# Squares summed as they arise, h made in pieces and halved HGRN exponents in a hybrid SSD / HGRN2 / S5 / MoE layer

## The chip, the cores and the metric

The kernel runs on one core of a Trainium2 chip. The metric is device time in microseconds (us) for one call. The core's engines work side by side, each through its own instructions in order, and wait for each other on semaphores: PE (TensorE, matrix products and transposes), DVE (VectorE), ACT (ScalarE), POOL (GpSimd), and SP, which here only issues DMA transfers. All data is float32. PE's records come in pairs: one 128x320 product in the program is two MATMUL records in the trace.

## The reference, cut to what matters

One layer, with 256 prompt tokens and 64 sample tokens of width 2048, 320 in all. The parts that this change touches:

```python
def rmsnorm(x, g):
    xf = x.astype(F32)
    y = xf * lax.rsqrt(jnp.mean(xf * xf, axis=-1, keepdims=True) + EPS)
    return (y * g.astype(F32)).astype(x.dtype)

# chunk_gla, 64 tokens per chunk; HGRN has a decay per key, SSD one per head
b = jnp.cumsum(lc, axis=1)
diff = b[:, :, None] - b[:, None, :]
dec = jnp.where(causal[...], jnp.exp(jnp.minimum(diff, 0.0)), 0.0)
scores = jnp.einsum('bthk,bshk,btshk->btsh', qc, kc, dec)        # HGRN

# mixer
y_a = y_a.reshape(bsz, t, SSD_WIDTH) * jax.nn.silu(z.astype(F32))
out_a = rmsnorm(y_a, P['ssd_norm_g'][l])                         # the SSD norm
merged = jnp.concatenate([out_a, out_b, out_c], axis=-1)
mix = merged @ P['w_out'][l]

# trunk
x = x + gt1 * m
h = rmsnorm(x, P['g_ffn'][l]) * (1 + sc2) + sh2                  # the second norm (n2)
x = x + gt2 * hmoe(h, P, l)                                      # router, 32 experts, top 2 of one group
```

## The kernel before, in words

Activations lie with channels on the partitions and the 320 tokens along the free dimension: `xT` and `hT` are 16 tiles of 128 x 320. A table, `PLAN`, written out by rules in `make_plan`, sets one order of work for PE, and from it `act_order` makes the order of ACT and DVE. The heavy input projections (L1066), the modulation products (L965) and the parts of the output projection that don't need SSD (L1099) are laid as filler between the steps of S5, HGRN and SSD, so that PE has something to do while DVE and ACT prepare a step. Since PE works strictly in order, a step whose operands come late stops the filler behind it too.

**HGRN.** Two pairs of heads, seven levels each. At level 0 a masked product of q and k gives the diagonal. At each of the levels m = 32, 16, 8, 4, 2, 1 (`hg_level`) the tokens fall into blocks of 2m; only pairs with the query in a block's later half and the key in its earlier half count, and a mask (`lmask`) drops all others. DVE makes, over all 640 columns (two heads x 320), the difference of the running sum `hb` to the block's reference column (L1772) and the smaller of it and its negative (L1773); ACT takes the exponential (L781); DVE multiplies q (L1776) and k (L1777) with it, and PE forms the scores (L1172).

**SSD.** Five chunks of 64 tokens. For each, PE makes the decays (L1263, `ssd_decay`), DVE and ACT the weights, and PE the output (L1271, L1282, L1287, `ssd_y`). DVE gates it into `proj`, tiles 0 to 7 (L1947, semaphore `ssd_done`). When all five are done, and POOL has added the last filler piece to `xT` (`x_part` 16), ACT squares the eight tiles two at a time into the two halves of `sq` (L673) while PE sums them over the partitions with a matrix of ones (`sum_squares`, L956). DVE makes the mean (L1537), ACT the root, DVE the reciprocal (L1541) and the normed tiles (L1954).

**Output projection and second norm.** PE then runs 16 tiles of 8 products (L1345) with four PSUM banks in rotation; after each tile DVE adds it to `xT` (L2001, `x_mixed`). ACT squares pairs of tiles of `xT` into `sq`, which has two places. They are released by PE's `sum_squares`, and that stands behind the whole output projection. After it come the mean, the root, the reciprocal, four small operations that make the scale (1 + sc2) g (L1552, L1553, `modulate`), four multiplications of four tiles each (L1546, `scale_x`), and the shift: ACT does the prompt columns of each tile (L684), DVE the 64 sample columns (L1557). The router's 16 products (L1354) each need one finished tile of `hT`. Behind them follow the choice of experts, the gather of tokens, and 16 pairs of experts, whose weights SP loads as places come free.

## Time and profile before

| | us |
|---|---|
| median of 3 runs | 1496.92 (1494.64 to 1498.01) |
| the profiled execution's own time | 1496.93 |
| its span in the trace | 1495.0 |
| PE busy | 1224.5 (82%) |
| DVE busy | 520.3 (35%) |
| ACT busy | 197.6 (13%) |
| POOL busy | 261.6 (18%) |

The share of each engine is an average over stages with different limits. HGRN lies between about 381 and 634 us, SSD between 636 and 765, the output projection from 765 to 837, the second norm and the router from 837 to 869, the choice of experts up to 904, and the experts from 904 to 1406. The time outside the span is 1.9 us.

### The profile page before, as it was taken

The numbers are of one execution on the slowest core, as the hardware profiler recorded it, in microseconds if no ns is written. First come the engines' busy times: TensorE is split into PE (matmuls) and PEld (weight loads), VectorE is DVE, ScalarE is ACT, GpSimd is POOL, SyncE is SP. The second block draws the span as 40 slices with busy tenths as digits, with TensorE's granted clock in tenths as the row PEclk, the third lists the DMA queues.
The fourth block names the chain that finished last, engine by engine and source line by source line (L and its number), as shares of the span: only waits on it lengthen the run. The fifth ranks groups of instructions, "written<-read, shape, count | busy, mean of one in ns | idle before, by whom it ended". The sixth has DMA issues, their size and how long they took to land.

```text
span 1495.0 us, 14778 instructions
## 1 busy us (share of the span) xinstructions
PE 1224.5 (82%) x5914; PEld 664.9 (44%) x5914; DVE 520.3 (35%) x1020; ACT 197.6 (13%) x319; POOL 261.6 (18%) x568
## 2 busy tenths in 40 slices
PE   4799999989998778989979768787878777877625
PEld 2346555545555445656657444233323222333224
DVE  1412575644563673246621441111211111111054
ACT  1311011010211310132210320000000000000011
POOL 4170288881000000021120000000001000000010
PEclk9899899989998889899989878999999988999857
DMA  9998668675574636332123526999999999999432
GB/s 341 368 359 301 211 225 281 234 273 172 185 274 159 235 105 234 127 95 91 57 71 121 216 72 243 420 421 417 416 410 391 409 403 416 398 413 409 175 138 71
DMA packets 140085, 387.01 MB, mean 259 GB/s; under 512 B 15211, under 2 KB 54501, under 8 KB 112558
## 3 DMA queue, kind: packets, MB, share of 16 engines
q1 hardware_dynamic: 132208, 361.91, 64.2%
q0 software_dynamic: 6528, 18.72, 3.6%
q10 hardware_dynamic: 1280, 5.42, 1.0%
q8 instruction: 48, 0.79, 0.2%
q14 instruction: 21, 0.17, 0.0%
HBM read 385.95 MB, written 23.13 MB: 274 GB/s over the span
## 4 chain that ended last, share of the span: by engine, by line
PE 45%; DMA 26%; DVE 10%; POOL 10%; issue 3%; ACT 2%; SPq 2%; DVEq 0%; POOLq 0%; ACTq 0%
DMA slot<-in_w_exp_up 21%; PE psum L1411 11%; PE psum L1066 10%; PE psum L1345 5%; PE psum L1099 4%; DMA slot<-in_w_ada 4%; PE psum L995 3%; PE psum L965 2%; PE psum L956 2%; POOL mem L540 2%; POOL sq L541 2%; POOL sq L538 2%; POOL mem L543 2%; POOL sq L542 1%; POOL sq L539 1%
## 5 line engine op out<-in xcount | busy, mean ns | idle before, releaser
L1411 PE MATMUL psum<-slot,mem 128*64 128x512 f32 x1024 | 258.8, 664 | 83.4 <-DMA slot<-in_w_exp_up 82.5
L1066 PE MATMUL psum<-hT,slot 128*128 128x320 f32 (+1 forms) x1056 | 308.3, 452 | 0.0
L1066 PEld LDWEIGHTS psum<-hT,slot 128*128 128x128 f32 (+1 forms) x1056 | 204.5, 196 | 100.3 <-issue 27.9
L1411 PEld LDWEIGHTS psum<-slot,mem 128*64 128x64 f32 x1024 | 85.7, 153 | 255.2 <-issue 171.4
L2128 DVE TENSOR_TENSOR sq<-sq,psum 128x256 f32<-128x256 f32 x16 | 6.7, 422 | 380.7 <-ACT sq L911 380.7
L1435 PE MATMUL psum<-mem,sq 128*64 128x512 f32 x512 | 113.4, 594 | 8.6 <-issue 7.1
L965 PE MATMUL psum<-slot,cT 128*8 128x512 f32 (+1 forms) x768 | 98.9, 629 | 21.1 <-DMA slot<-in_w_ada 20.9
L610 POOL DMA_INDIRECT moe_output<-mem,idx x16 | 16.2, 1011 | 483.6 <-ACT mem L915 483.6
L1345 PE MATMUL psum<-mem,slot 128*128 128x320 f32 x256 | 71.9, 445 | 5.4 <-DVE mem L1954 5.4
L1099 PE MATMUL psum<-mem,slot 128*128 128x320 f32 x256 | 75.2, 450 | 0.0
L1435 PEld LDWEIGHTS psum<-mem,sq 128*64 128x64 f32 x512 | 41.9, 137 | 69.9 <-issue 68.7
L1345 PEld LDWEIGHTS psum<-mem,slot 128*128 128x128 f32 x256 | 50.1, 196 | 27.2 <-issue 7.5
L1099 PEld LDWEIGHTS psum<-mem,slot 128*128 128x128 f32 x256 | 49.5, 198 | 24.0 <-issue 5.8
L1398 PE MATMUL psum<-ident,mem 128*128 128x128 f32 x256 | 38.7, 287 | 16.2 <-DVE mem L2118 9.0
L911 ACT ACTIVATE sq<-psum 128x256 f32<-128x256 f32 x16 | 6.1, 384 | 342.2 <-PE psum L1411 342.2
L965 PEld LDWEIGHTS psum<-slot,cT 128*8 128x8 f32 (+1 forms) x768 | 16.9, 89 | 71.5 <-issue 65.9
L2118 DVE COPY mem<-psum 128x512 f32<-128x512 f32 x64 | 42.6, 685 | 8.4 <-PE psum L1398 8.3
L1398 PEld LDWEIGHTS psum<-ident,mem 128*128 128x128 f32 x256 | 29.3, 145 | 32.0 <-issue 30.0
L956 PE MATMUL psum<-sq,ones 128*128 128x320 f32 x112 | 36.1, 485 | 7.0 <-ACT sq L673 6.1
L616 POOL DMA_INDIRECT mem<-moe_input,idx x16 | 16.4, 1027 | 139.0 <-DMA moe_input<-mem 134.5
L558 POOL DMA_DIRECT2D out_hgrn_p<-mem x1 | 0.8, 782 | 222.7 <-DVE mem L1809 222.7
L995 PE MATMUL psum<-hT,mem 128*128 128x320 f32 x128 | 38.3, 451 | 1.0 <-ACT hT L684 1.0
(426 smaller groups left out, 1301.1 us busy)
## 6 DMA issues: line engine op xcount, KB each, us to landing
slot<-in_w_ada SPq DMA_DIRECT2D x48, 2048.0 KB, 11.0
slot<-in_w_exp_gate SPq DMA_DIRECT2D x64, 1024.0 KB, 14.7
slot<-in_w_exp_up SPq DMA_DIRECT2D x64, 1024.0 KB, 16.9
mem<-in_w_exp_down SPq DMA_DIRECT2D x32, 2048.0 KB, 17.5
slot<-in_w_in SPq DMA_DIRECT2D x17, 2048.0 KB, 11.8
slot<-in_w_out SPq DMA_DIRECT2D x8, 2048.0 KB, 8.4
mem<-in_w_in SPq DMA_DIRECT2D x2, 2048.0 KB, 18.4
mem<-in_x_prompt ACTq DMA_DIRECT2D x1, 2048.0 KB, 12.4
```

What stands on the lines that cost most here:

```text
L538: pl(g.tensor_tensor(tt[:, :, 0:m], pc[:, :, 0:m], cm, ALU.mult))
L540: pl(g.tensor_tensor(pc[:, :, m:2 * m], tt[:, :, 0:m], t2[:, :, 0:m], ALU.subtract))
L956: last = mm(bank(b, T), ones[:, :], sq[:, i % 2, q * T:q * T + T], start=(i == 0 and q == 0), stop=(i == count - 1 and q == 1))
L965: done = mm(psum[32 * c:32 * c + width, 2, :], cT[:, 8 * h + kk, lo:lo + width], w[:, kk, :], start=(first and kk < 4), stop=(last and kk ...
L995: last = mm(bank(EARLY_BANK[e], T), w[:, k, q * P:(q + 1) * P], hT[:, k, :], start=(k == 0), stop=(k == KD - 1))
L1066: last = mm(psum[0:wd, grp % 2, 0:T], w[:, k, q * P:q * P + wd], hT[:, k, :], start=(k == 0), stop=(k == KD - 1))
L1099: last = mm(bank(grp % 2, T), w[:, k, q * P:(q + 1) * P], mixed[8 + k], start=(k == 4), stop=(k == 3))
L1345: last = mm(bank(4 + m % 4, T), w[:, k, q * P:(q + 1) * P], mixed[k], start=(k == 0), stop=(k == 7))
L1398: last = tr(bank(6 + g_ % 2, P, lo=q * P), xg[par][:, (4 * g_ + q) * P:(4 * g_ + q + 1) * P], ident[:, :])
L1411: last = mm(psum[rows_, 0, :].rearrange("p (w n) -> p w n", w=2), xe[i % 2][:, k, rows_], gate_up[h][:, :, k, :], start=(k == 0), stop=(k ...
L1435: last = mm(psum[rows_, 1 + n, :], aTT[:, f, rows_], dn[h][:, f, 512 * n:512 * n + 512], start=(f == 0), stop=(f == 1))
L2118: v.tensor_copy(xe[par][:, 4 * g_:4 * g_ + 4, :], bank(6 + g_ % 2).rearrange("p (k t) -> p k t", k=4))\
```

## The change

It has four parts.

- **SSD norm.** ACT squares each chunk of 64 columns of all eight tiles (512 columns per partition) into `hT`, which is free by then: chunk c at the start of the step `ssd_decay(c + 1)`, the last in `ssd_norm`. PE sums the first four chunks (eight products of 256 columns) right behind the decays of the fifth, into bank 2, and the fifth (eight products of 64 columns) at the end. ACT no longer waits there for `x_part`; that wait now stands in front of the squares of `xT`.
- **Second norm.** DVE copies the first pair's squares to `sum_sq` (a part of `BDT`) and adds the next six there as they come, behind every second tile of the output projection; this also releases the places of `sq`. PE sums `sum_sq` and the eighth pair at the end: 4 products instead of 16.
- **h in pieces.** The four small operations for the scale go in front of the output projection. `scale_x` makes pieces of 1, 1, 2, 4, 4 and 4 tiles, with their sample shifts behind each piece.
- **HGRN.** At each level the difference is made with the right sign for each half (later: `hb` minus reference; earlier: reference minus `hb`), and q is multiplied in the later halves only, k in the earlier ones. What stands in the other halves falls under the mask; `hk_` is zeroed once.

```diff
-NORM = {"n1": 0, "ssd": 8, "n2": 12, "n3": 20}
+NORM = {"n1": 0, "ssd": 8, "n2": 13, "n3": 21}
...
+        sum_sq = BDT[:, :, :, :].rearrange("p w u n -> p (w u n)")[:, 0:2 * T]
...
+            def chunk_squares(c):
+                cols = slice(c * CH, c * CH + CH)
+                act.wait_ge(S("ssd_done"), c + 1)
+                st(s.activation(hT[:, 0:8, cols], proj[:, 0:8, cols], ACT.Square), "squares")
+
             def ssd_decay(c):
                 half = slice(CH * (c % 2), CH * (c % 2) + CH)
+                if c:
+                    chunk_squares(c - 1)
...
             def ssd_norm():
-                act.wait_ge(S("ssd_done"), NCH)
-                act.wait_ge(S("x_part"), 16)
-                for i in range(4):
-                    squares(proj[:, 2 * i:2 * i + 2, :], i, "ssd")
+                chunk_squares(NCH - 1)
...
+            act.wait_ge(S("x_part"), 16)
             for i in range(8):
                 act.wait_ge(S("x_mixed"), 4 * (i + 1))
                 squares(xT[:, 2 * i:2 * i + 2, :], i, "n2")
...
-                shift_prompt(3, k, 4 + k // 4 + 1)
+                shift_prompt(3, k, 4 + (1, 2, 3, 3, 4, 5, 6)[k if k < 4 else 3 + k // 4])
...
+                if c == NCH - 1:
+                    pe.wait_ge(S("squares"), NORM["ssd"] + 4)
+                    for k in range(8):
+                        last = mm(bank(2, TP), ones[:, :], hT[:, k, 0:TP], start=(k == 0), stop=(k == 7))
+                    last.then_inc(S("squares_used"), 4)
...
-                    sum_squares(3, 4, "ssd")
+                    pe.wait_ge(S("squares"), NORM["ssd"] + 5)
+                    for k in range(8):
+                        last = mm(bank(2, TS, lo=TP), ones[:, :], hT[:, k, TP:T], start=(k == 0), stop=(k == 7))
+                    last.then_inc(S("squares_used"), 1)
...
-            sum_squares(3, 8, "n2")
+            pe.wait_ge(S("squares_used"), NORM["n2"] + 7)
+            for q in range(2):
+                mm(bank(3, T), ones[:, :], sum_sq[:, q * T:q * T + T], start=(q == 0), stop=False)
+            pe.wait_ge(S("squares"), NORM["n2"] + 8)
+            for q in range(2):
+                last = mm(bank(3, T), ones[:, :], sq[:, 1, q * T:q * T + T], start=False, stop=(q == 1))
+            last.then_inc(S("squares_used"), 1)
...
+                if hp == 0:
+                    st(v.memset(hk_, 0.0))
...
-                b3 = hb3(hb, m)
-                st(tt(hb3(hE, m), b3, bc(b3[:, :, m - 1:m], [P, 640 // (2 * m), 2 * m]), SUB))
-                st(stt(hE, hE, -1.0, hE, MUL, ALU.min), "hg_expo")
+                early, later = (slice(0, m), slice(m, 2 * m))
+                b3, e3 = hb3(hb, m), hb3(hE, m)
+                ref = bc(b3[:, :, m - 1:m], [P, 640 // (2 * m), m])
+                st(tt(e3[:, :, later], b3[:, :, later], ref, SUB), wait=False)
+                st(tt(e3[:, :, early], ref, b3[:, :, early], SUB), "hg_expo")
                 hg_take(hp, lv - 1)
                 dve.wait_ge(S("hg_exp"), 6 * hp + lv)
-                st(tt(hq_, q_, hE, MUL))
-                st(tt(hk_, k_, hE, MUL), "hg_qk")
+                st(tt(hb3(hq_, m)[:, :, later], hb3(q_, m)[:, :, later], e3[:, :, later], MUL), wait=False)
+                st(tt(hb3(hk_, m)[:, :, early], hb3(k_, m)[:, :, early], e3[:, :, early], MUL), "hg_qk")
...
-                mean_square(3, 1024)
+                mean_square(2, 1024)
...
             dve.wait_ge(S("mod_ready"), 12)
-
+            for s_ in range(2):
+                st(ts(ab1[:, :, s_], seg(4)[:, :, s_], 1.0, None, ADD))
+                st(tt(ab1[:, :, s_], ab1[:, :, s_], g_ffn, MUL))
...
+                if m % 2 and m > 1:
+                    i = m // 2 - 1
+                    dve.wait_ge(S("squares"), NORM["n2"] + i + 1)
+                    if i == 0:
+                        st(v.tensor_copy(sum_sq, sq[:, 0, :]), "squares_used", wait=False)
+                    else:
+                        dve.wait_ge(S("squares_used"), NORM["n2"] + i)
+                        st(tt(sum_sq, sum_sq, sq[:, i % 2, :], ADD), "squares_used", wait=False)
...
-            modulate(g_ffn, 4)
-            for k in range(KD):
-                shift_sample(3, k)
+            for k, n in ((0, 1), (1, 1), (2, 2), (4, 4), (8, 4), (12, 4)):
+                scale_x(k, n)
+                for kk in range(k, k + n):
+                    shift_sample(3, kk)
```

The next pieces show the order of instructions of one engine (names are output <- inputs, then the shape). First DVE at the first and second HGRN level of the first pair of heads, before:

```order
L1772 TENSOR_TENSOR mem<-mem 128x640
L1773 SCALAR_TENSOR_TENSOR mem<-mem 128x640
L1762 TENSOR_TENSOR mem<-psum,lmask 128x384
L1776 TENSOR_TENSOR mem<-mem 128x640
L1777 TENSOR_TENSOR mem<-mem 128x640
L1772 TENSOR_TENSOR mem<-mem 128x640
L1773 SCALAR_TENSOR_TENSOR mem<-mem 128x640
```

and now, where L1790 and L1791 make the two halves of the difference, L1778 takes the scores of the level ahead, and L1794 and L1795 are the products with q and k:

```order
L1790 TENSOR_TENSOR mem<-mem 128x10x32
L1791 TENSOR_TENSOR mem<-mem 128x10x32
L1778 TENSOR_TENSOR mem<-psum,lmask 128x384
L1794 TENSOR_TENSOR mem<-mem 128x10x32
L1795 TENSOR_TENSOR mem<-mem 128x10x32
L1790 TENSOR_TENSOR mem<-mem 128x20x16
L1791 TENSOR_TENSOR mem<-mem 128x20x16
```

The number of instructions is the same; each of the four now covers 320 columns instead of 640.

PE from the last chunk's decays (L1263) to the router (L1354), before:

```order
L1263 MATMUL psum<-mem,ones 128x512 x2
L1099 MATMUL psum<-mem,slot 128x320 x8
L1271 MATMUL psum<-mem 64x512 x2
L1282 MATMUL psum<-mem 64x64 x16
L1287 MATMUL psum<-mem 64x64 x16
L1099 MATMUL psum<-mem,slot 128x320 x8
L956 MATMUL psum<-sq,ones 128x320 x8
L1345 MATMUL psum<-mem,slot 128x320 x128
L956 MATMUL psum<-sq,ones 128x320 x16
L1354 MATMUL psum<-hT,mem 36x320 x16
```

and now (L1271 the decays, L1284 to L1300 the chunk's output, L1361 the output projection, L1376 the router):

```order
L1271 MATMUL psum<-mem,ones 128x512 x2
L1276 MATMUL psum<-hT,ones 128x256 x8
L1107 MATMUL psum<-mem,slot 128x320 x8
L1284 MATMUL psum<-mem 64x512 x2
L1295 MATMUL psum<-mem 64x64 x16
L1300 MATMUL psum<-mem 64x64 x16
L1107 MATMUL psum<-mem,slot 128x320 x8
L1345 MATMUL psum<-hT,ones 128x64 x8
L1361 MATMUL psum<-mem,slot 128x320 x128
L1365 MATMUL psum<-BDT,ones 128x320 x2
L1368 MATMUL psum<-sq,ones 128x320 x2
L1376 MATMUL psum<-hT,mem 36x320 x16
```

The sum over the first four chunks has moved ahead of two filler pieces and the chunk's output; behind the last filler only 8 products of 64 columns are left, and behind the output projection 4 of 320.

DVE between the reciprocal and the clearing of the router's table, before:

```order
L1541 RECIPROCAL rinv<-rinv 128x320
L1552 TENSOR_SCALAR ab<-modT 128x16
L1553 TENSOR_TENSOR ab<-ab,parT 128x16
L1552 TENSOR_SCALAR ab<-modT 128x16
L1553 TENSOR_TENSOR ab<-ab,parT 128x16
L1546 TENSOR_TENSOR hT<-xT,rinv 128x1280 x4
L1557 TENSOR_SCALAR hT<-hT,ab,modT 128x64 x16
L2014 MEMSET mem 128x512
```

and now:

```order
L2030 TENSOR_TENSOR BDT<-BDT,sq 128x640
L1559 TENSOR_SCALAR rinv<-psum 128x320
L1563 RECIPROCAL rinv<-rinv 128x320
L1566 TENSOR_TENSOR hT<-xT,rinv 128x320
L1569 TENSOR_SCALAR hT<-hT,ab,modT 128x64
L1566 TENSOR_TENSOR hT<-xT,rinv 128x320
L1569 TENSOR_SCALAR hT<-hT,ab,modT 128x64
L1566 TENSOR_TENSOR hT<-xT,rinv 128x640
L1569 TENSOR_SCALAR hT<-hT,ab,modT 128x64 x2
L1566 TENSOR_TENSOR hT<-xT,rinv 128x1280
L1569 TENSOR_SCALAR hT<-hT,ab,modT 128x64 x4
L1566 TENSOR_TENSOR hT<-xT,rinv 128x1280
L1569 TENSOR_SCALAR hT<-hT,ab,modT 128x64 x4
L1566 TENSOR_TENSOR hT<-xT,rinv 128x1280
L1569 TENSOR_SCALAR hT<-hT,ab,modT 128x64 x4
L2043 MEMSET mem 128x512
```

The scaling (L1566) and the sample shifts (L1569) now take turns in growing pieces, and the four small operations on `ab` are gone from here.

## Rows read from the trace of the kernel before

**Rows 1.** The chain that ended last: start us, us, what.

```profile
765.30 71.89 PE psum L1345 x256
...
837.19 8.92 PE psum L956 x32
...
856.96 11.78 PE psum L1354 x32
...
945.35 25.77 DMA slot<-in_w_exp_up
```

**Rows 2.** PE's waits from 370 to 760 us: total us, times, longest.

```profile
PE psum L1172 <- DVE mem L1777: 20.1, 4, 14.6
```

**Rows 3.** Timeline, first HGRN level: start, us, engine, operation [idle before].

```profile
393.11 0.82 DVE L1772 TENSOR_TENSOR mem<-mem 128x640 f32<-128x640 f32 x1
...
397.40 0.92 PE L1172 MATMUL psum<-mem 128*64 128x64 f32 x24 [3.06 <-DVE mem L1777]
```

**Rows 4.** Timeline, PE's waits at two later HGRN levels.

```profile
530.63 1.55 PE L1172 MATMUL psum<-mem 128*64 128x64 f32 x24 [14.61 <-DVE mem L1777]
...
557.96 0.92 PE L1172 MATMUL psum<-mem 128*64 128x64 f32 x24 [1.21 <-DVE mem L1777]
```

**Rows 5.** DVE instructions by line and shape, 370 to 870 us.

```profile
L1772 DVE TENSOR_TENSOR mem<-mem 128x640 f32<-128x640 f32 x12 | 9.9, 825 | 0.4
...
L1821 DVE TENSOR_TENSOR mem<-mem 128x320 f32<-128x320 f32 x4 | 2.0, 492 | 0.1
...
L1546 DVE TENSOR_TENSOR hT<-xT,rinv 128x1280 f32<-128x1280 f32 x4 | 6.0, 1493 | 0.1
```

**Rows 6.** Timeline, last SSD chunk to its norm.

```profile
735.69 4.57 PE L1099 MATMUL psum<-mem,slot 128*128 128x320 f32 x16
...
742.74 1.34 PE L1282 MATMUL psum<-mem 64*64 64x64 f32 x32 [1.47 <-DVE mem L1920]
...
751.02 0.68 ACT L826 ACTIVATE sq<-psum,modT 128x256 f32<-128x256 f32 x2 [9.99 <-PE psum L1099]
...
753.52 6.34 PE L956 MATMUL psum<-sq,ones 128*128 128x320 f32 x16 [2.54 <-ACT sq L673]
...
755.90 0.74 ACT L673 ACTIVATE sq<-mem 128x640 f32<-128x640 f32 x1 [1.66 <-PE psum L956]
...
759.97 0.49 DVE L1537 TENSOR_SCALAR rinv<-psum 128x320 f32<-128x320 f32 x1 [12.46 <-PE psum L956]
```

**Rows 7.** Timeline, four narrow matmuls with 128 columns of weights.

```profile
634.60 0.95 PE L1084 MATMUL psum<-small,rows 128*128 128x8 f32 x8
```

**Rows 8.** Timeline, output projection's end to the router matmuls.

```profile
828.61 0.68 DVE L2001 SCALAR_TENSOR_TENSOR xT<-psum,modT,xT 128x256 f32<-128x256 f32 x2 [3.63 <-PE psum L1345]
...
846.21 0.49 DVE L1537 TENSOR_SCALAR rinv<-psum 128x320 f32<-128x320 f32 x1 [8.30 <-PE psum L956]
...
847.36 2.15 DVE L1541 RECIPROCAL rinv<-rinv 128x320 f32<-128x320 f32 x1 [0.66 <-ACT rinv L888]
...
849.55 0.18 DVE L1552 TENSOR_SCALAR ab<-modT 128x16 f32<-128x16 f32 x1
...
851.98 7.97 ACT L684 ACTIVATE hT<-hT,modT,ab 128x256 f32<-128x256 f32 x16 [4.72 <-DVE hT L1546]
...
856.50 3.66 DVE L1557 TENSOR_SCALAR hT<-hT,ab,modT 128x64 f32<-128x64 f32 x16
...
856.96 11.77 PE L1354 MATMUL psum<-hT,mem 128*36 128x320 f32 x32 [10.86 <-DVE hT L1557]
```

**Rows 9.** Windows, PE alone: us, busy (x), granted clock, DMA share, GB/s.

```profile
846.10:849.40 3.30, 0.00 (x0) 0.99 0.99 420
...
849.40:857.00 7.60, 0.04 (x1) 0.50 0.57 241
...
857.00:863.00 6.00, 6.00 (x12) 0.50 0.00 0
...
863.00:868.70 5.70, 5.70 (x22) 1.00 0.01 3
```

More of the change, by code:

```diff
@@ L1541, in invert, with scale_x @@
                 st(v.reciprocal(rinv[:, :], rinv[:, :]))
-            def scale_x():
-                dve.wait_ge(S("x_transposed"), 12)
-                for k in range(0, KD, 4):
-                    st(tt(hT[:, k:k + 4, :], xT[:, k:k + 4, :], bc(rinv[:, :].unsqueeze(1), [P, 4, T]), MUL),
-                       "h_scaled")
-            def modulate(g, sc):
-                for s_ in range(2):
-                    st(ts(ab1[:, :, s_], seg(sc)[:, :, s_], 1.0, None, ADD))
-                    st(tt(ab1[:, :, s_], ab1[:, :, s_], g, MUL))
-                scale_x()
+            def scale_x(k, n):
+                st(tt(hT[:, k:k + n, :], xT[:, k:k + n, :], bc(rinv[:, :].unsqueeze(1), [P, n, T]), MUL), "h_scaled")
             def shift_sample(sh, k):
@@ L1583, in _ @@
             invert(("root", 1))
-            scale_x()
+            dve.wait_ge(S("x_transposed"), 12)
+            for k in range(0, KD, 4):
+                scale_x(k, 4)
             first_shift(0)
@@ L1949, in ssd_norm @@
             def ssd_norm():
-                dve.wait_ge(S("squares_used"), NORM["ssd"] + 4)
-                mean_square(3, 1024)
+                dve.wait_ge(S("squares_used"), NORM["ssd"] + 5)
+                mean_square(2, 1024)
                 invert(("root", 2))
```

## The prediction

> **What bounds the kernel now.** I read the page's sums first, then the chain that ended last in order of time, then PE's waits and the timeline at the places that the change touches. The sums (PE 82%, DVE 35% busy) say nothing of a single edit. The chain does: from 765.30 to 904 us it goes through the output projection, the sum of the squares of `xT`, the norm, the router and the choice of experts, one after another, and from about 940 us on it alternates between expert weights landing and PE [rows 1]. In the expert stage nothing starts by the clock on the wall: SP issues each load when PE has used up the one before, so whatever is saved ahead of 904 us moves the whole stage forward. Before 765 us PE is the bound and works in order; the only places where it waits for the HGRN operations of the change are four, 20.1 us in all, the longest 14.6 [rows 2].
>
> **HGRN halves.** Per level DVE loses none of its four instructions, but each covers 320 columns instead of 640. A TENSOR_TENSOR of 640 takes 0.825 us and one of 320 takes 0.492 [rows 5], so a pair falls by 2 x 0.333 = 0.67. Twelve levels make 12 x 1.33 = 16 us of DVE time, but nearly all of it lies beside PE's filler. What counts are the four waits. At the first level of each head pair the difference (from 393.11) and the products stand in one chain that PE waits for (wait before 397.40; 14.61 before 530.63) [rows 3, 4]: 2 x 0.67 = 1.33 each. At two later levels (1.21 each; one of them before 557.96 [rows 4]) the difference has been made ahead and only the products count: 0.67 each. Sum 1.33 x 2 + 0.67 x 2 = **4.0 us**. All four waits are longer than that, so the whole gain reaches PE, and the filler behind it waits for nothing else in this stretch. The clearing of `hk_` (640 columns, at most the 0.825 of a two-operand pass) stands ahead of DVE's wait for the sigmoids, where DVE has nothing to do; nothing on the path. No row shows an operation on halves with gaps between them. If it costs as much as the whole, the gain is 0; if the price were strictly per column (0.41), 5.0. I take 4.0, since the 320-column row is the nearest. Levels with the shortest runs (m = 2, 1) are not at a wait.
>
> **SSD norm.** Before, the last filler piece ends at 750.98; then come the evacuation (0.68), POOL's addition, the first squares, PE's sums from 753.52 to 759.86, and DVE's mean at 759.97 [rows 6]. So 9.0 us lie between the filler's end and the mean. Now: evacuation 0.68, square of 512 columns (at most the 0.74 of a 640-column one [rows 6]), 8 products of 64 columns. These are 16 records with 128 columns of weights; the nearest row is 8 such records with 8 columns, 0.95 us or 0.12 each [rows 7], and I take 0.16 for 64 columns: 2.6 us. With four hand-overs of some 0.07: 4.2 us. Gain 9.0 - 4.2 = 4.8. Against it stands what is moved forward on PE: 8 products of 256 columns behind the decays of the last chunk, 16 records x 0.281 (71.89 us / 256 [rows 1]) x 256 / 320 = 3.6 us. They push the filler piece at 735.69, and PE had 1.47 us of waiting before 742.74 to absorb them [rows 6]; the rest, 2.1 to 2.3 us, delays the chunk's output and everything behind it. Net **2.5 us**. ACT's squares of the earlier chunks (0.7 us each) stand behind an evacuation and ahead of exponentials whose argument DVE makes only after `ssd_done`; ACT is idle there. Bounds: 0 if the 64-column records run at half clock, as the sums from 753.52 partly do; 5.9 if PE's insertion were all absorbed and the short records took 0.08.
>
> **Squares of xT.** Before, ACT's squares from the third pair on wait for PE behind the output projection: PE sums until 846.11 while the projection ended at 837.19, and the mean starts at 846.21 [rows 1, 8]. Now ACT squares each pair as it comes, and DVE adds it: 0.83 us for 640 columns on top of 0.68 for each second tile. DVE waits 3.63 us for PE in front of every tile [rows 8], so the addition is hidden. At the end: last addition to `xT` (0.68 from 837.23) to 837.91; ACT's last square (0.74) and DVE's last addition (0.83) side by side to 838.8; 4 products of 0.56 to 841.1. Gain 846.1 - 841.1 = **5.0 us**; bounds 4.0 (a pause puts the last 4 products at half clock) and 5.5.
>
> **h in pieces, scale ahead.** Count from the end of the reciprocal, 849.51 (847.36 + 2.15). Before, the router's products started at 856.96 and ended at 868.73: 19.2 us behind it [rows 8]. Of these, 0.84 went to the four small operations, 6.1 to the four multiplications (1.49 each [rows 5]), then 3.66 for 16 sample shifts (0.23 each) and 7.97 for 16 prompt shifts on ACT (0.50 each) [rows 8]. Now DVE's pieces end at 0.5, 1.3, 2.5, 4.5, 7.0 and 9.5 us, with shifts between, all done at 10.5 (6.4 + 3.7 + gaps). ACT has tile 0 at 1.1, tile 4 at 5.1, tile 8 at 7.6, tile 12 at 10.1, tile 15 at 11.6. PE starts at 1.2. If it then needs the same 11.77 us, it ends at 12.9; if the clock stayed high, operands would bound it: 11.6 plus a handover and one product, 12.2. PE's clock was 0.99 while PE stood idle until 849.4, 0.50 from there until 863, 6 us into the router's products, and 1.00 after [rows 9]; I take 12.8, since the present pause of 10.9 us becomes 4.6 but the stretch starts at most a little warmer. Gain 19.2 - 12.8 = **6.4 us**, the four small operations included; these hide in front of DVE's first wait for the output projection.
>
> **Sum.** 4.0 + 2.5 + 5.0 + 6.4 = 17.9 us. The profiled execution took 1496.93 us (span 1495.0), the median of the three runs is 1496.92, so both give 1496.9 - 17.9 = **1479.0 us**, 1.2% faster. Nothing behind the router's products changes, and no load comes earlier than its place: the first expert pair's loads follow the output projection and are over by 854 us [DMA share 0.57 until 857, then 0.00, rows 9], some 50 us before they are used, so they cannot hold up a router that is 14 us earlier.
>
> **The rivals.**
> *A. Strided halves bring nothing, or the inserted sums eat the SSD gain.* Terms 1 and 2 have no row of their own kind. Without HGRN's 4.0: 1483.0; without both: 1485.5. For it speaks only the missing row; against it that the chain's waits are there and the 320-column row is direct. Chance 0.15.
> *B. PE's clock stays at 1.2 GHz for all router products.* They now stop for operands at each piece. With the whole stretch at the slow level, 12 records per 6.0 us [rows 9] rather than 22 per 5.7: 32 records take at least 16 us, so the end comes 17 to 18 us behind the reciprocal and the gain of that term is 1.5: 1483.9. Against it: at the slow level PE itself is slower than the pieces come (1.0 us a tile against 0.6 to 0.9), so it has no pauses in which to stay cold. Chance 0.08.
> [...]
> *C. The gain is given back in the expert stage.* If the stage were bound by a supply of weights that runs on by itself, saving ahead of it would be lost: 1496.9. Against it: DMA share 0.00 from 857 on; the loads wait for PE. Chance 0.03.
> *D. Slower: DVE becomes the bound of the output projection.* It has 4.31 us per tile (0.68 + 3.63), 8.6 per pair, and uses 1.36 + 0.83 = 2.2. Its addition waits, in order, for ACT's square, and behind it stands the next tile's `x_mixed`, for which PE waits four tiles later. It decides from 8.6 us a pair; at 12 us a pair the eight pairs cost 8 x 3.4 = 27 us more, less the 17.9: 1506. ACT's squares take 0.74 and depend on tiles two steps back, so I see nothing that brings it there. Chance 0.03.
>
> **How the numbers follow.** The forecast has 0.71, A 0.15, B 0.08, C 0.03, D 0.03. Its own range takes half the distance to the ends of the unknown terms: HGRN 2 to 5, SSD 1 to 5, squares 4.5 to 5.3, router 5.5 to 7: 13 to 22 us, less likely together, so 1476 to 1483. For 8 in 10 I add most of A and B above: **1475.5 to 1485**. A measurement of this kernel can tell about 0.2%, 3 us, from no change. Forecast, A and B are all faster by more (0.94), C is the same (0.03), D slower (0.03).
>
> **What would show it.** HGRN: DVE's four operations at 0.49 us, PE's wait before the level at 530 near 13.3 instead of 14.6, the two of 1.21 near 0.5. SSD: a block of 256-column products of 3.6 us behind the last decays; from the last filler's end to the mean about 4.2 instead of 9.0. Squares: mean about 4 us behind the projection's end (9.0 before), and DVE still waiting over 2 us for PE before each tile. Router: first product 1.2 us and last 12.8 us behind the reciprocal, clock low in the first half. Experts: the stage from the first expert product to the last unchanged at about 500 us. I am wrong if a half costs more than 0.6 us, if the chunk's output is delayed by more than 4 us, or if the expert stage grows by what was saved.

## The result and the profile after

| | before | after |
|---|---|---|
| median | 1495.78 us (4 runs, 1494.16 to 1498.01) | 1473.76 us (4 runs, 1472.09 to 1476.12) |
| the profiled execution's own time | 1496.93 | 1472.83 |
| its span in the trace | 1495.0 | 1471.0 |
| PE busy | 1224.5 | 1215.5 |
| DVE busy | 520.3 | 505.5 |

The ratio of after to before is 0.9853 (95%: 0.9832 to 0.9874): 22 us or 1.5% faster. The forecast was 1479.0 with a range from 1475.5 to 1485. The sign was right, but the gain is 22.0 us between the medians and 24.0 between the spans, not 17.9, and the time lies below the range. The forecast was counted from 1496.9; from the median of before in this table, 1495.78, it would have been 1477.9, so 1.1 us of the distance in the time is the starting point's and not the change's. Two executions of e3 below, 1507.64 and 2460.07 us, were slow ones and stand in no median or ratio here.

To find where the time went I cut both traces at the same instructions. A cut stands at the start of a record: of the first one where a stage begins, of the last one where it ends (so "the last filler product" below is cut 0.4 us before its end). Lengths are in us; behind the stroke stands how many of them had PE granted 1.2 GHz (0.50 in the profile's clock) instead of 2.4.

| stretch | before | after | difference | predicted |
|---|---|---|---|---|
| start to S5's gate | 362.5 | 365.2 | +2.7 | 0 |
| S5's gate to the last chunk's decays (HGRN in it) | 372.7 / 61.4 | 366.8 / 61.4 | -5.9 | -4.0 |
| decays to the last filler product | 15.4 / 3.4 | 15.6 / 0 | +0.2 | +2.1 to 2.3 |
| to the SSD mean | 9.4 / 3.4 | 3.8 / 0 | -5.6 | -4.8 |
| to the output projection | 5.3 | 5.4 | +0.1 | 0 |
| output projection | 71.5 / 5.6 | 70.3 / 3.3 | -1.2 | 0 |
| to the mean of the second norm | 9.4 | 4.5 | -4.9 | -5.0 |
| to the router's last product | 22.1 / 13.7 | 15.8 / 6.8 | -6.3 | -6.4 |
| to the first expert product | 35.9 | 35.9 | 0.0 | 0 |
| experts | 508.1 | 507.2 | -0.9 | 0 |
| last expert product to the end | 82.7 | 80.5 | -2.2 | 0 |

The first row and the last two are not of the change. Its code doesn't touch them, and over all kernels profiled they scatter without order: the first takes 362.5 us in before, the shortest of all, and 363.3 to 367.4 in the others, the experts 506.7 to 510.5, the end 80.5 to 83.4. What is of the change sums to 23.6 us in this pair of traces.

**HGRN.** The four halves, grouped by line and shape (line, engine, operation, shapes, count; then busy us and mean ns):

```profile
L1794 DVE TENSOR_TENSOR mem<-mem 128x320 f32<-128x320 f32 x12 | 5.9, 493 | 0.9 <-ACT mem L783 0.6
L1790 DVE TENSOR_TENSOR mem<-mem 128x320 f32<-128x320 f32 x12 | 5.9, 492 | 0.4
L1791 DVE TENSOR_TENSOR mem<-mem 128x320 f32<-128x320 f32 x12 | 5.8, 484 | 0.0
L1795 DVE TENSOR_TENSOR mem<-mem 128x320 f32<-128x320 f32 x12 | 5.8, 484 | 0.0
```

So a half with gaps costs what 320 dense columns cost [rows 5]. PE's waits between 370 and 760 us (waited for: total, times, longest), which answer to [rows 2]:

```profile
PE psum L1180 <- DVE mem L1795: 15.8, 4, 13.5
PE psum L1192 <- DVE mem L1807: 8.3, 2, 4.1
```

And the first level and the waits at the second pair in PE's timeline (start, us, engine, line, what; in brackets the idle time before it and what ended it), answering to [rows 3, 4]:

```profile
395.15 1.90 PE L973 MATMUL psum<-slot,cT 128*8 128x512 f32 x16
398.54 0.92 PE L1180 MATMUL psum<-mem 128*64 128x64 f32 x24 [1.48 <-DVE mem L1795]
399.39 8.88 PE L1074 MATMUL psum<-hT,slot 128*128 128x320 f32 x32
...
529.09 1.55 PE L1180 MATMUL psum<-mem 128*64 128x64 f32 x24 [13.47 <-DVE mem L1795]
530.57 9.62 PE L1074 MATMUL psum<-hT,slot 128*128 128x320 f32 x27
...
556.13 0.92 PE L1180 MATMUL psum<-mem 128*64 128x64 f32 x24 [0.42 <-DVE mem L1795]
```

The waits fell by 1.58, 1.14 and twice 0.79: 4.3 us, against 4.0 predicted. The filler behind the first level went from 10.57 us to 8.88; its row before was:

```profile
398.25 10.57 PE L1066 MATMUL psum<-hT,slot 128*128 128x320 f32 x32
```

**SSD norm.** From the last chunk's decays to the output projection, answering to [rows 6]:

```profile
732.49 3.72 PE L1276 MATMUL psum<-hT,ones 128*128 128x256 f32 x16
...
736.05 4.47 PE L1107 MATMUL psum<-mem,slot 128*128 128x320 f32 x16
...
740.45 1.08 PE L1284 MATMUL psum<-mem 64*64 64x512 f32 x4
...
741.36 1.10 PE L1295 MATMUL psum<-mem 64*64 64x64 f32 x32
...
742.39 1.15 PE L1300 MATMUL psum<-mem 128*64 128x64 f32 x32
...
743.47 4.57 PE L1107 MATMUL psum<-mem,slot 128*128 128x320 f32 x16
...
748.65 0.63 ACT L836 ACTIVATE hT<-mem 128x512 f32<-128x512 f32 x1
...
749.33 2.00 PE L1345 MATMUL psum<-hT,ones 128*128 128x64 f32 x16 [1.29 <-ACT hT L836]
...
751.44 0.49 DVE L1559 TENSOR_SCALAR rinv<-psum 128x320 f32<-128x320 f32 x1 [5.65 <-PE psum L1345]
```

The inserted products cost 3.72 us of PE, as priced (3.6). But the wait of 1.47 us in the chunk's output is gone whole, and the rows behind it ran at full clock: the output's last rows took 1.15 us where they had taken 1.97, and the last filler 4.57 where it had taken 5.07. Counted from the last decays, the output's first 64-column record starts 1.8 us later than before (9.4 against 7.6), the last filler 0.8 later, and its last record only 0.2. These are the two rows of before, which follow that of 742.74 in [rows 6]:

```profile
744.01 1.97 PE L1287 MATMUL psum<-mem 128*64 128x64 f32 x32
745.91 5.07 PE L1099 MATMUL psum<-mem,slot 128*128 128x320 f32 x16
```

**Second norm and router**, answering to [rows 8]:

```profile
827.60 0.67 DVE L2021 SCALAR_TENSOR_TENSOR xT<-psum,modT,xT 128x256 f32<-128x256 f32 x2 [3.63 <-PE psum L1361]
828.19 0.81 DVE L2030 TENSOR_TENSOR BDT<-BDT,sq 128x640 f32<-128x640 f32 x1
...
829.05 1.34 PE L1365 MATMUL psum<-BDT,ones 128*128 128x320 f32 x4 [1.50 <-DVE BDT L2030]
830.23 1.24 PE L1368 MATMUL psum<-sq,ones 128*128 128x320 f32 x4
831.58 0.49 DVE L1559 TENSOR_SCALAR rinv<-psum 128x320 f32<-128x320 f32 x1 [2.58 <-PE psum L1368]
...
832.74 2.15 DVE L1563 RECIPROCAL rinv<-rinv 128x320 f32<-128x320 f32 x1 [0.66 <-ACT rinv L896]
...
836.21 11.65 PE L1376 MATMUL psum<-hT,mem 128*36 128x320 f32 x32 [4.74 <-ACT hT L686]
```

The mean comes 4.5 us behind the start of the projection's last record (9.4 before), or 4.0 behind its end (9.0). The router starts 1.3 us behind the reciprocal's end (834.89) and ends 13.0 behind it, 1.2 and 12.8 predicted. DVE still waits 3.63 us for PE ahead of a tile, so the additions are hidden. Windows of PE (window; its length, PE busy, granted clock, DMA share, GB/s), the first at the end of the long HGRN wait, the others in the router, answering to [rows 9]:

```profile
529.00:531.00 2.00, 1.91 (x25) 0.50 0.00 0
...
836.20:839.00 2.80, 2.79 (x6) 0.50 1.01 427
839.00:841.00 2.00, 2.00 (x6) 0.50 1.03 434
841.00:843.00 2.00, 2.00 (x7) 0.74 0.98 414
843.00:848.00 5.00, 4.86 (x19) 1.00 0.24 97
```

The router starts at 1.2 GHz and rises within the stretch, as before, though loads now run beside it (DMA share 1.01); they cost it nothing that shows (11.65 us against 11.77).

### The profile page after: what moved, and what is told of

Same layout as the page of the kernel before. It is cut to its first block, busy times and chain, and to the rows that moved or that the text cites. A ratio compares the mean times of both kernels' runs of the same rounds, so it can differ in the third digit from the quotient of the medians.

```text
span 1471.0 us, 14779 instructions
## 1 busy us (share of the span) xinstructions
PE 1215.5 (83%) x5906; PEld 660.0 (45%) x5906; DVE 505.5 (34%) x1030; ACT 197.5 (13%) x320; POOL 262.2 (18%) x568
## 4 chain that ended last, share of the span: by engine, by line
PE 45%; DMA 26%; POOL 10%; DVE 9%; issue 3%; SPq 3%; ACT 2%; DVEq 0%; POOLq 0%; ACTq 0%
DMA slot<-in_w_exp_up 21%; PE psum L1433 11%; PE psum L1074 10%; PE psum L1361 5%; PE psum L1107 4%; DMA slot<-in_w_ada 3%; PE psum L1003 3%; PE psum L973 3%; POOL mem L542 2%; POOL sq L540 2%; POOL mem L545 2%; POOL sq L543 2%; POOL sq L544 2%; POOL sq L541 2%; SPq L433 1%
## 5 line engine op out<-in xcount | busy, mean ns | idle before, releaser
L973 PE MATMUL psum<-slot,cT 128*8 128x512 f32 (+1 forms) x768 | 102.1, 640 | 16.3 <-DMA slot<-in_w_ada 16.3
L1361 PE MATMUL psum<-mem,slot 128*128 128x320 f32 x256 | 70.8, 440 | 5.4 <-DVE mem L1972 5.4
L1361 PEld LDWEIGHTS psum<-mem,slot 128*128 128x128 f32 x256 | 49.5, 194 | 26.3 <-issue 6.3
L1107 PEld LDWEIGHTS psum<-mem,slot 128*128 128x128 f32 x256 | 49.1, 196 | 23.6 <-issue 5.5
L923 ACT ACTIVATE mem<-psum 128x1024 f32<-128x1024 f32 x16 | 16.4, 1024 | 162.1 <-PE psum L1457 162.1
## 6 DMA issues: line engine op xcount, KB each, us to landing
slot<-in_w_exp_gate SPq DMA_DIRECT2D x64, 1024.0 KB, 13.7
```

What stands on the lines that cost most here:

```text
L973: done = mm(psum[32 * c:32 * c + width, 2, :], cT[:, 8 * h + kk, lo:lo + width], w[:, kk, :], start=(first and kk < 4), stop=(last and kk ...
L1107: last = mm(bank(grp % 2, T), w[:, k, q * P:(q + 1) * P], mixed[8 + k], start=(k == 4), stop=(k == 3))
L1361: last = mm(bank(4 + m % 4, T), w[:, k, q * P:(q + 1) * P], mixed[k], start=(k == 0), stop=(k == 7))
```

## The experiments

All ratios are to the kernel before, timed on the same chip; e9 and e10 ran on another chip than the rest, so their times are compared by ratio. Two theories stand against each other from e5 on. By the *pricing* theory a stretch costs its instructions plus its waits, and the clock is a given. By the *clock* theory a pause of PE can also bring on a stretch at 1.2 GHz near it, so a pause costs more than its length, and work put into it costs less than its price.

### One part alone: e1 to e4

Each kernel is the one before plus one part of the diff shown ahead of the prediction, the other lines as before. e1 has the SSD norm alone, e2 the squares of the second norm, e3 the pieces of `h` with the scale ahead, e4 the HGRN halves.

```diff
 # e1 keeps these lines of the change and none of the others
+                if c:
+                    chunk_squares(c - 1)
+                    pe.wait_ge(S("squares"), NORM["ssd"] + 4)
...
 # e4 keeps these
+                st(tt(e3[:, :, later], b3[:, :, later], ref, SUB), wait=False)
+                st(tt(e3[:, :, early], ref, b3[:, :, early], SUB), "hg_expo")
```

> The kernel before with the SSD norm's part alone (chunk squares on ACT, the sums in two parts). Theory 1 (what the trace after shows from the last chunk's decays to the mean: the products put in fill PE's wait for W and leave its clock high): 5.3 us faster up to the mean, filler's end to mean 3.4 us, and 0 to 1 us more from the output projection's clock, so 1489.5 to 1491. Theory 2 (the prediction's term: the products put in delay the chunk's output by 2.1 us): 2.5 us faster, 1493.5.

> The kernel before with the second norm's squares summed on DVE beside the output projection, alone. Both theories: projection's end to mean 4.0 us instead of 9.0, so 5.0 us faster, about 1491. Rival: DVE's additions slow the projection: its 71.9 us grow.

> The kernel before with the scale made ahead and h in growing pieces, alone. Prediction's term: 6.4 us faster, about 1489.5, the router's last product 12.8 us behind the reciprocal. Rival (the pause in front of it is longer here, since PE's sums end earlier relative to nothing): the same first product, 1.2 us behind the reciprocal, so no difference in the gain. If the clock stayed low through all products, 1.5 us faster only.

> The kernel before with the halved HGRN exponents alone. Prediction's term: the four waits of PE fall by 4.0 us in sum, to about 16, and the kernel by 4.0, about 1491.8. Rival (shorter waits also leave PE's clock high in the filler behind them, and what the comparison after-before shows beyond the 17.9 us comes from here): 6 us or more faster.

| | median us | ratio (95%) | the part's own stretch, before | alone | in the whole change |
|---|---|---|---|---|---|
| e1 SSD norm | 1492.99 | 0.9988 (0.9965 to 1.0011) | 24.8 | 19.5 | 19.4 |
| e2 squares of `xT` | 1491.36 | 0.9984 (0.9963 to 1.0004) | 9.4 | 4.4 | 4.5 |
| e3 `h` in pieces | 1487.17 | 0.9962 (0.9937 to 0.9987) | 22.1 | 15.7 | 15.8 |
| e4 HGRN | 1491.52 | 0.9975 (0.9956 to 0.9993) | 372.7 | 366.6 | 366.8 |

The stretches are those of the first table: decays to mean, projection to mean, mean to the router's last product, S5's gate to the last decays. Each part gives in its own stretch what it gives in the whole change, to 0.2 us: 6.4 for `h`, 6.1 for HGRN, 5.3 for SSD, 5.0 for the squares. The HGRN stretch is 372.7 to 374.0 us in the five traces with the old code there, and 366.4 to 367.3 in the five with the new one and no products added there, so its gain is 6 us with a scatter of about one. In the others' stretches the clock moves: e4, which touches nothing behind HGRN, takes 17.0 us instead of 15.4 from the last decays to the filler's end (6.8 of them slow instead of 3.4) and 70.3 instead of 71.5 in the projection (3.3 slow instead of 5.6), and e1 takes 70.7 there. e2 and e3 keep 71.5. So the projection's 1.2 us don't come from the edit of the second norm, which stands inside it, but with those of HGRN and SSD ahead of it, and the HGRN part alone gives 1.6 us back at the end of SSD, which only the filled wait of the SSD part takes away again.

The whole times don't resolve this. The kernel before itself ran from 1486.62 to 1502.28 us on this chip (34 executions), and an interval of a ratio spans 4 to 5 per mille, which is 5.5 to 7.5 us. The four ratios leave 9.1 per mille in all (13.6 us), where the stretches sum to 22.8 us; the whole change, timed on the same chip (e8 below), leaves 13.9 per mille. The half-widths of the four intervals, squared and added, make about 4.4 per mille, so the distance from 9.1 to 13.9 is about as large as the noise of both, while that to the 22.8 us of the stretches (15.3 per mille) is a little larger than the noise. For e1 the stretch's gain (5.3 us, 3.5 per mille) lies at the edge of the interval; its median, 1492.99, is nearer to the 1493.5 of its second theory than to the 1489.5 to 1491 of the first, though from filler to mean the trace has what the first said. e4's median is 1.5 us below that of before, where 4 or 6 were expected. What of a single part's gain is lost in such stretches, what in the stages behind (in e3 the experts took 2.4 us longer), and what is chance, these runs don't tell.

### e5: the four chunks' sums at the end instead of behind the decays

```diff
@@ behind the last decays
-                if c == NCH - 1:
-                    pe.wait_ge(S("squares"), NORM["ssd"] + 4)
-                    for k in range(8):
-                        last = mm(bank(2, TP), ones[:, :], hT[:, k, 0:TP], start=(k == 0), stop=(k == 7))
-                    last.then_inc(S("squares_used"), 4)
@@ in ssd_norm, ahead of the eight products of 64 columns
+                    pe.wait_ge(S("squares"), NORM["ssd"] + 4)
+                    for k in range(8):
+                        last = mm(bank(2, TP), ones[:, :], hT[:, k, 0:TP], start=(k == 0), stop=(k == 7))
+                    last.then_inc(S("squares_used"), 4)
```

> The kernel after, but the eight products over the first four chunks' squares stand at the end, right ahead of the eight of the last chunk, instead of behind the last chunk's decays. Prediction's pricing (put in early they cost 3.6 less the 1.47 us of waiting they fill, 2.1; at the end 3.6): 1.5 us slower than the kernel after between the last decays and the mean. Clock theory (put in early they cost 0.2 us, since they fill the wait and leave no slow spell): 3.4 us slower at least, and PE again at the slow level somewhere between the last decays and the mean.

Measured: 1480.45 us, ratio 0.9884 (0.9849 to 0.9918). PE's timeline of e5 from the last decays on:

```profile
734.37 4.57 PE L1107 MATMUL psum<-mem,slot 128*128 128x320 f32 x16
738.88 1.08 PE L1279 MATMUL psum<-mem 64*64 64x512 f32 x4
741.42 1.97 PE L1290 MATMUL psum<-mem 64*64 64x64 f32 x32 [1.47 <-DVE mem L1937]
743.32 1.97 PE L1295 MATMUL psum<-mem 128*64 128x64 f32 x32
745.23 6.06 PE L1107 MATMUL psum<-mem,slot 128*128 128x320 f32 x16
751.13 3.62 PE L1340 MATMUL psum<-hT,ones 128*128 128x256 f32 x16
754.58 1.90 PE L1344 MATMUL psum<-hT,ones 128*128 128x64 f32 x16
```

The wait of 1.47 us is back, and behind it both halves of the output take 1.97 us and the filler 6.06: 10.0 us for rows that take 6.8 in after (1.10, 1.15, 4.57). From decays to mean it is 22.7 us against 19.4. The expectation took the sums' whole 3.6 us as the price of the late place, and so 1.5 us by pricing. The rows show less: at the end the sums start at once behind the filler, while ACT evacuates it and squares the last chunk, so they fill PE's wait of 1.29 us there, and the tail grows by 1.9 us only. By pricing the two places then cost nearly the same, 2.1 us early and 1.9 late. The early one was better by 3.3, and the rows behind the wait, which do the same work at the other clock level, differ by 3.2. (17.0 us from the decays to the filler is also what e4 has, with no sums moved at all; in before it is 15.4, with the same wait of 1.47 us but 3.4 slow us instead of 6.8. So a wait of one length didn't always cost the same.)

### e9: the same products put into the kernel before, unread

This takes the rest of the change away. Eight products of 256 columns, whose result nobody reads, stand behind the last decays of the kernel before; the work is extra.

```diff
+                if c == NCH - 1:
+                    for k in range(8):
+                        mm(bank(2, TP), ones[:, :], hT[:, k, 0:TP], start=(k == 0), stop=(k == 7))
```

> The kernel before with eight products of 256 columns added behind the last chunk's decays; nobody reads them, and the SSD norm's own sums stay as they were. Clock theory: from the last decays to the last filler 15.4 becomes 15.6 us though 3.6 us of products were added, PE is at the high level there, and the norm's 16 old products run faster too (filler to mean about 7.7 instead of 9.4 us). Prediction's pricing: 2.1 us longer up to the last filler, nothing after.

Measured (one execution, 1498.17 us, where the kernel before took 1487.99 to 1500.7, which says nothing about the time). PE's timeline:

```profile
736.50 3.72 PE L1267 MATMUL psum<-hT,ones 128*128 128x256 f32 x16
740.06 4.47 PE L1099 MATMUL psum<-mem,slot 128*128 128x320 f32 x16
744.46 1.08 PE L1274 MATMUL psum<-mem 64*64 64x512 f32 x4
745.37 1.10 PE L1285 MATMUL psum<-mem 64*64 64x64 f32 x32
746.40 1.15 PE L1290 MATMUL psum<-mem 128*64 128x64 f32 x32
747.48 4.57 PE L1099 MATMUL psum<-mem,slot 128*128 128x320 f32 x16
754.59 6.34 PE L956 MATMUL psum<-sq,ones 128*128 128x320 f32 x16 [2.53 <-ACT sq L673]
```

3.72 us of extra work moved the last filler product by 0.2 us (15.4 to 15.6 from the decays), with every row up to it at full clock, as in after. This is the point that the sum had wrong, and it is shown without the rest of the change. The other half of what I expected, that the sums at the end would run faster too, fell: from filler to mean it took 9.4 us as before, 3.4 of them slow, and 6.34 in the same sums. Of the two slow spells around the end of SSD the filled wait removed the one behind it and left the other.

### e6 and e7: PE's pauses filled with unread products

e6 is after plus 8 unread products of 320 columns in the pause behind the SSD sums and 7 in the pause behind the second norm's sums. e7 is e6 plus 22 in the long HGRN wait and 6 ahead of each of the two waits for the keys' transposes.

```diff
             pe.wait_ge(S("bulk_evac"), ALL_GROUPS)
+            for k in range(8):
+                mm(bank(0, T), ones[:, :], hT[:, k, :], start=(k == 0), stop=(k == 7))
...
+            for k in range(7):
+                mm(bank(1, T), ones[:, :], sum_sq[:, 0:T], start=(k == 0), stop=(k == 6))
             pe.wait_ge(S("router_loaded"), 64)
@@ e7 only
+            def keep_busy(n):
+                for k in range(n):
+                    mm(bank(3, T), ones[:, :], hT[:, k % KD, :], start=(k == 0), stop=(k == n - 1))
...
+                    if hp == 1 and lv == 1:
+                        keep_busy(22)
                     pe.wait_ge(S("hg_qk"), 6 * hp + lv)
...
+                keep_busy(6)
                 pe.wait_ge(S("hg_kd"), hp + 1)
```

> The kernel after with products added that nobody reads: 8 of 320 columns behind the SSD norm's sums, in PE's pause before the output projection (5.4 us), and 7 in the pause before the router (4.7 us). Clock theory: the slow spell at the start of the output projection (3.3 us there in the kernel after) and in the router's products (5.9 us) goes; projection 68.7 instead of 70.3 us, router's products about 10.5 instead of 11.2 (operands bound it), 2 us faster than the kernel after. Rival (slow spells follow from the load as a whole, not from the pauses): no stage changes, or the added products push the real ones: 0 to 1 us slower.

> As the last one, and also 22 products of 320 columns in PE's 13.5 us wait at the first level of the second head pair, and 6 in each of the two 4.1 us waits for the keys (hg_kd). Clock theory: of the 34 us at the slow level between the S5 gate and the last HGRN scores 10 to 20 go, each worth half: 5 to 10 us faster than the kernel after in that stretch, besides the 2 us of the last one. Rival: nothing there, or some 1 us slower.

Measured: e6 1471.13 us, ratio 0.9828 (0.9796 to 0.9859); e7 1467.12, ratio 0.9794 (0.976 to 0.9827). The windows of the output projection and of the router, of e6:

```profile
757.50:826.20 68.70, 68.70 (x256) 1.00 0.27 98
835.30:846.20 10.90, 9.65 (x32) 1.00 0.73 307
```

and the output projection of after:

```profile
756.80:827.10 70.30, 70.30 (x255) 0.98 0.26 96
```

The projection loses 1.6 us and the router 0.8, at clock 1.00 throughout. The median is 5.3 us below that of the changed kernel on the same chip (e8 below), more than the 2.4 of these two stretches; where the rest comes from isn't shown. In the router PE now waits for its operands, three times:

```profile
835.28 1.37 PE L1380 MATMUL psum<-hT,mem 128*36 128x320 f32 x4 [0.97 <-ACT hT L686]
837.00 1.27 PE L1380 MATMUL psum<-hT,mem 128*36 128x320 f32 x4 [0.35 <-ACT hT L686]
838.98 7.18 PE L1380 MATMUL psum<-hT,mem 128*36 128x320 f32 x24 [0.71 <-ACT hT L686]
```

so operands bound it at full clock, as the prediction had said of that case (12.2 us behind the reciprocal; the clock bounds it otherwise). In e7 the long HGRN wait is nearly all work:

```profile
513.43 12.11 PE L1153 MATMUL psum<-hT,ones 128*128 128x320 f32 x44
526.47 0.92 PE L1186 MATMUL psum<-mem 128*64 128x64 f32 x24 [0.93 <-DVE mem L1806]
527.32 8.88 PE L1074 MATMUL psum<-hT,slot 128*128 128x320 f32 x32
```

The scores behind it take 0.92 us instead of 1.55 and the filler 8.88 for 32 products. From S5's gate to the last HGRN scores it is 205.3 us, of which 6.8 are slow, against 212.8 and 34.1 in after: 7.5 us from products whose result nobody reads. No instruction of the kernel's own was changed, and the rows above are the same records at the other clock level, so the clock is the cause.

The time confirms it: all six executions of e7 (1462.1 to 1469.11 us) lie below all six of e8 (1474.41 to 1477.11), and the medians are 9.3 us apart. Not all of the HGRN stretch's gain is in the step from e6, though: from e6 to e7 that stretch lost 7.8 us, the medians 4.0 and the spans 3.8. In e7's trace the start is 1.9 us longer and the end 2.4 (83.4, and 83.2 in e10, the longest two). Whether that is the scatter of those stretches or a price of the extra work isn't settled.

### e8: the changed kernel again

Unchanged, beside e5 to e7 on the same chip.

> The kernel after once more, unchanged, on the same chip as the three above, to see what its stages differ by from one execution to another. Theory 1 (the terms of the comparison are those of the change): stage lengths from 362 us to the router's end repeat within 1 us, and the ratio to before is again near 0.985. Rival (part of the 22 us was chance): the ratio is near 0.988, as the prediction's 17.9 us would give.

Measured: 1476.45 us, ratio 0.9861 (0.983 to 0.9892). Its stretches repeat those of after to 0.2 us up to the router: from S5's gate to the last HGRN scores 212.6, to SSD's first decays 67.7, to the last decays 86.3, then as in the first table 15.7, 3.8, 5.3, 70.3 and 4.5, to the router's first product 4.6 and to its last 11.2. So in these two executions the slow spells come at the same places.

### e10: more pauses filled

e7 plus 8 unread products ahead of the token transposes of the routing, 10 ahead of the first gathered tokens, and 50 behind the last expert pair.

```diff
+                if g == 4:
+                    keep_busy_late(8)
...
             pe.wait_ge(S("act_rows"), 12)
+            keep_busy_late(10)
...
+            for k in range(50):
+                mm(bank(0, T), ones[:, :], sum_sq[:, 0:T], start=(k == 0), stop=(k == 49))
```

> As the kernel with all pauses filled, and also 8 unread products ahead of the transposes that wait for the router's choice, 10 ahead of the first gathered tokens and 50 behind the last expert pair, where PE waits for the gather. Clock theory: router's end to first expert product 35.7 becomes 33 to 34 us, expert stage's first pair 1 to 2 us shorter, tail 82 becomes 78, so 4 to 7 us faster than with all pauses filled. Rival: these stages are bound by DVE, ACT and DMA; under 1 us.

Measured: 1465.28 us, ratio 0.9799 (0.9769 to 0.9828); e7's interval and this one overlap nearly whole, where 4 to 7 us more had been expected. From the router to the first expert product it took 34.4 us instead of 35.7, with 10.2 slow instead of 20.5, so ten microseconds of slow clock were worth 1.3: in this stretch PE mostly waits for others. The expert stage, whose first pair was expected to be 1 to 2 us shorter, took 1.4 us longer as a whole (508.1 against 506.7). Behind the experts nothing changed (83.2 against 83.4), though PE's slow time there fell from 61.7 to 34.3 us: what lies behind the last expert pair isn't set by PE's clock. By ratio e7 and e10 are the fastest kernels of this study, both ahead of the change itself.

## Why the prediction was right in kind and short in size

**Right, as worked out.** The squares of `xT`: 5.0 predicted, 4.9 measured, alone and in the whole. `h` in pieces: 6.4 predicted, 6.3 measured; the clock of the router's products was taken right, too (low at first, full in the second half). HGRN's waits: 4.0 predicted, 4.3 measured, and the choice of the 320-column row (0.49 us) for halves with gaps was the right one of its two ends.

**The SSD norm was mis-sized: 2.5 predicted, 5.4 measured** (5.3 in e1). Two parts of that term failed.
1. "The rest, 2.1 to 2.3 us, delays the chunk's output and everything behind it": the output did start 1.8 us later, but the last filler product only 0.2. I had subtracted the wait of 1.47 us from 3.6 us of products, and kept the durations behind it as they were. But the row of the chunk's output, 1.97 us for 32 short records, and the filler's 5.07 were slow *because of* where PE had stood idle; with the wait filled they took 1.15 and 4.57. e5 (wait back: 3.3 us slower) and e9 (wait filled in the kernel before: 0.2 us for 3.72 us of work) show it.
2. The tail: 16 records of 64 columns took 2.00 us, 0.125 each, where I took 0.16 (2.6 us). From the filler's end to the mean it was 3.4 us, not the 4.2 of the sum, where the old one was 9.0: a gain of 5.6 instead of 4.8.

The term's upper bound, 5.9, held what was measured; I chose a value near the middle.

**A term was missing: the clock elsewhere.** In the stretch with HGRN, beyond its waits, PE was busy 1.7 us less with the same products (334.0 to 332.4 us in all); the filler behind the first level went from 10.57 to 8.88 us. In the output projection 1.2 us went the same way. Together 2.8 us that no edit had a price for. The slow time itself didn't shrink in either place. In the HGRN stretch it is 61.4 us in both traces, but PE was at work in 47.7 of them before and in 44.3 after; half of that difference is the 1.7. Around the start of the projection there is one slow spell of 6.8 us in both: before, it began 1.3 us ahead of the first product, after, 3.5 us ahead, in PE's pause, where it costs nothing. So in this pair the 2.8 us come from where the spells fell and not from less of them. They recur in e8, and in length in e4, where only HGRN is changed; its spell at the projection is 3.4 us long (in e5 and e6 PE's busy time fell less, but then the long wait was shorter too, and the stretch took as long). e6 and e7 show that what is left, 1.6 us in the projection and 7.5 in HGRN, can be had by filling pauses. Why the spells moved as they did no run shows; that they moved to the kernel's good is luck as far as the prediction goes, which had nothing on them.

The sum by measured terms is 5.9 + 5.4 + 1.2 + 4.9 + 6.3 = 23.7 us, 0.1 less for the step to the projection, which makes the 23.6 of the stretches. The medians give 22.0 and the spans 24.0; a spread of 1 to 2 us between them is that of the parts which the change doesn't touch.

**The rivals.** A (halves or insertion bring nothing): no, 0.49 us a half, and 0.2 us of delay. B (the router at 1.2 GHz throughout): no, 6.8 slow us behind the mean and then full clock. In e6 there were three waits of 0.35 to 0.97 us inside a stretch that stayed at clock 1.00; behind the waits of 13.5 us (HGRN) and 4.74 us (router) of after the clock was 0.50. The Trainium skill (TensorE: Matmul & The Clock Gate, HAM oscillation — how this bites in real kernels) tells of a kernel with about 2 us of products between waits of some 3 to 5 us, whose products start at the low clock behind every wait. The two long waits here agree with that; the router's short ones are not of that kind, so that case doesn't speak for B. C (given back in the experts): no, 508.1 to 507.2. D (DVE the bound of the projection): no, it waits as long as before.

**The range.** Its lower end, 1475.5, stood for 21.4 us of gain. The prediction said that it took half the distance to each term's end, but its upper values (5, 5, 5.3 and 7) are nearly the ends themselves; they sum to 22.3, or 1474.6, and it then shortened this to 1476 "less likely together". The measured time, 1473.76, lies below even the 1474.6, since no term stood for the clock in HGRN and in the projection. The terms weren't independent either: where PE's slow spells fell pushed three stretches the same way. And nearly all the room given outside the forecast's own case lay on the slow side, for A and B.

None of the signs of being wrong that the prediction named was seen (a half above 0.6 us, an output more than 4 us late, a longer expert stage). All three looked for a loss; a gain beyond the range had no sign.

## What to carry over

A wait in front of PE can cost more than its own length, because the rows behind it may run slow. So before pricing work that is moved into a wait, compare the rows behind the wait with rows of the same shape elsewhere (here 1.97 against 1.15 us, 5.07 against 4.57): their difference may be part of the gain, and it belongs on the fast side of the range. Where a kernel has a few long waits of PE that can't be shortened, products that nobody reads are worth a try; here 49 of them took the changed kernel from 1476.45 to 1467.12 us, or from 0.9861 to 0.9794 of the kernel before.

## What the runs showed of the chip

- An operation of DVE on every second run of m columns costs what a dense one of as many columns costs: 0.48 to 0.49 us for 320, at each level from runs of 32 down to runs of 1 column.
- Filling a pause removed the slow spell behind it, not the next one: in e9 the output and the filler ran at full clock, and the sums 3 us behind them took 6.34 us as before. In e7 the slow time from S5's gate to the last HGRN scores fell from 34.1 to 6.8 us.
- A short pause didn't always bring a slow spell: behind the 1.47 us in SSD's last output the rows were slow in before, e4 and e5, but behind the 1.48 us ahead of the first HGRN level the rows of after ran at full clock (0.92 and 8.88 us). The length of the pause alone doesn't tell which.
- The slow spells mostly recur: after and e8 have 34.1 slow us in that stretch and 3.3 in the projection, both. Of the five traces whose code there is that of before, three have 34.1 (before, e2, e9) and two 37.5 (e1, e3). They behave more like a part of the schedule than like noise, but not wholly so.
- Sixteen records of 64 columns with 128 columns of weights run at 0.125 us each at full clock, hardly more than the 0.12 of 8 columns [rows 7].
